# Hybrid decoder step on one core: TensorE's order within an expert step, gathered row's sums ahead of the front piece

## The reference, cut to what matters

```python
q, k, v, u = project(x, w_in)
a = diff_attention(q, k, v, ...)        # 4 heads, causal; the sample group reads 8 pages of cached K and V a sequence
s = s5_mixer(u, ...)                    # state space model, then a gated linear unit (GLU)
x1 = layer_norm(ALPHA * x + concat(a, s) @ w_out)
# PEER: per token 8 heads, each picks 16 of 16384 experts
q = rms_norm(x1 @ w_q); s = q @ sub_keys; best, idx = top-k of sums of two top-16 lists
act = gelu(einsum('thkd,td->thk', u_tab[idx], x1))
f = einsum('thk,thkd->td', softmax(best) * act, v_tab[idx])
y = layer_norm(ALPHA * x1 + f)
```

## Time and profile before

| | |
|---|---|
| median of 3 runs | 3472.05 us (3468.49 to 3473.14) |
| profiled execution | 3468.09 us, of it span 3466.3 us |
| PE busy | 2588.0 us (75%) |
| DVE busy | 2387.7 us (69%) |
| ACT busy | 1510.9 us (44%) |
| POOL busy | 1258.6 us (36%) |
| mean granted TensorE clock | 0.821 |
| gathers (POOL, L1139) | 1088 of 1 MB, 1140.92 MB of 1314.04 MB moved |
| chain that ended last | DMA 32%, PE 26%, DVE 24%, ACT 8%, issue 7% |

### The profile page before, as it was taken

The page is one execution under the profiler, slowest core; times in us unless marked ns, Lnnn a source line. Parts: engine busy times, 40 slices in busy tenths (PEclk is TensorE's granted clock), DMA queues, the critical chain, the costliest instruction groups (busy, mean ns, idle before and its releaser), DMA issues.

```text
span 3466.3 us, 44430 instructions
## 1 busy us (share of the span) xinstructions
PE 2588.0 (75%) x14196; PEld 1078.2 (31%) x14196; DVE 2387.7 (69%) x5442; ACT 1510.9 (44%) x4355; POOL 1258.6 (36%) x1100
## 2 busy tenths in 40 slices
PE   8997897776777677767776687677767876778766
PEld 5664553321232123312331233123312322332311
DVE  8627754786678667876787678766876687446765
ACT  1124453435444444444444444544455444544443
POOL 0001343434443444344334443444344433224243
PEclk9998998877887778778877888789867986888966
DMA  5367999999999999999999999999999999999998
GB/s 162 82 184 289 387 416 373 421 383 420 418 421 386 417 421 417 389 415 421 421 385 415 421 421 383 410 421 418 386 406 421 409 386 401 359 381 380 415 364 336
DMA packets 245201, 1314.04 MB, mean 379 GB/s; under 512 B 50871, under 2 KB 72151, under 8 KB 94555
## 3 DMA queue, kind: packets, MB, share of 16 engines
q0 software_dynamic: 156672, 1140.92, 80.7%
q1 hardware_dynamic: 74576, 158.28, 12.5%
q10 hardware_dynamic: 13722, 12.01, 1.1%
HBM read 1291.83 MB, written 17.97 MB: 378 GB/s over the span
## 4 chain that ended last, share of the span: by engine, by line
DMA 32%; PE 26%; DVE 24%; ACT 8%; issue 7%; POOL 1%; SPq 1%; DVEq 0%; POOLq 0%; ACTq 0%
DMA UV<-in_peer_uv,zone_x 27%; PE psum L1363 10%; DVE zone_z L1721 10%; PE psum L389 3%; PE psum L1264 3%; PE psum L529 2%; DMA wq<-in_cache_k 2%; ACT L1474 2%; DVE zone_x L1618 1%; DVE zone_x L1619 1%; DVE zone_x L1621 1%; ACT D L1479 1%; DVE zone_x L1620 1%; ACT wge L1476 1%; ACT zone_y L1374 1%
## 5 line engine op out<-in xcount | busy, mean ns | idle before, releaser
L1139 POOL DMA_INDIRECT UV<-in_peer_uv,zone_x x1088 | 1253.0, 1152 | 2105.4 <-PE psum L1363 1763.9
L1363 PE MATMUL psum<-UV,D 64*64 64x512 f32 x8704 | 1431.1, 750 | 761.5 <-ACT D L1479 708.1
L1721 DVE CUSTOM_DVE_ANT_0 zone_z<-UV,zone_x 128x1024 bf16<-128x1024 f32 x1088 | 1333.7, 1226 | 711.1 <-DMA UV<-in_peer_uv,zone_x 647.7
L1474 ACT ACTIVATE ge<-acts 128x1 f32<-128x1 f32 x1088 | 219.3, 202 | 1456.8 <-DVE acts L1721 1452.6
L1363 PEld LDWEIGHTS psum<-UV,D 64*64 64x64 f32 x8704 | 301.0, 155 | 1537.2 <-issue 1470.0
L1479 ACT ACTIVATE D<-id,wge 128x64 f32<-128x64 f32 x1088 | 378.4, 348 | 35.4
L1476 ACT ACTIVATE wge<-ge,zone_x 128x1 f32<-128x1 f32 x1088 | 320.6, 295 | 35.4
L1293 PE MATMUL psum<-wq,zone_z 128*128 128x256 f32 x1024 | 288.6, 432 | 1.2 <-ACT zone_z L1415 1.2
L1293 PEld LDWEIGHTS psum<-wq,zone_z 128*128 128x128 f32 x1024 | 209.5, 215 | 149.7 <-issue 116.9
L1474 ACT ACT_TABLE_LOAD x115 | 147.5, 1283 | 2.4 <-ACT vrows L661 0.4
L1264 PE MATMUL psum<-w_out_sb,zone_z 128*128 128x512 f32 x256 | 128.8, 626 | 17.9 <-DMA w_out_sb<-in_w_out 17.9
(11 more groups left out here) (305 smaller groups left out, 2285.1 us busy)
## 6 DMA issues: line engine op xcount, KB each, us to landing
wq<-in_peer_w_q SPq DMA_DIRECT2D x72, 1024.0 KB, 9.5
UV<-in_peer_uv,zone_x POOLq DMA_INDIRECT x1088, 11.7
wq<-in_cache_k SPq DMA_DIRECT2D x64, 256.0 KB, 8.3
vrows<-in_cache_v SPq DMA_DIRECT2D x64, 256.0 KB, 6.0
wq<-in_w_in SPq DMA_DIRECT2D x11, 1024.0 KB, 5.4
zone_x<-in_x_all SPq DMA_DIRECT2D x9, 512.0 KB
UV<-in_w_out SPq DMA_DIRECT2D x2, 2048.0 KB, 12.3
w_out_sb<-in_w_out SPq DMA_DIRECT2D x1, 4096.0 KB, 17.7
```

What stands on the lines that cost most here:

```text
L1139: pool.indirect_dma_start(out=UV[:, n % RING, :], out_offset=None, in_=table, in_offset=bass.IndirectOffsetOnAxis(ap=icur[:, t % 2, k:k + ...
L1363: ins = pe.matmul(bank[6 + r][q:q + 64, :], D[64 * r:64 * r + 64, n % RING, :], UV[64 * r:64 * r + 64, n % RING, DM + 512 * e:DM + 512 * e ...
L1474: act.activation(ge[:, j:j + 1], acts[:, j:j + 1], ACT.Gelu).then_inc(sem("gelu_done"), 1)
L1721: dve.tensor_tensor_reduce(out=junk[:, :], in0=UV[:, n % RING, 0:DM], in1=x1[:, t % 2, :], scale=1.0, scalar=0.0, op0=ALU.mult, op1=ALU.ad ...
```

## The change

PE's body of an expert step is turned round: the sums of step k first, then the front pieces of step k. `pe_finish` and `pe_unit` still follow both. Nothing else changes: the same instructions, semaphores, slots and transfers, and the order on DVE, ACT, POOL and SP stays.

```diff
@@ -1838,9 +1838,9 @@
                     pe_front(pe, 0, f)
                 for t in range(NT + 1):
                     for k in range(steps(t)):
+                        pe_expert(pe, t, k)
                         for u, f in fronts(t, k):
                             pe_front(pe, u, f)
-                        pe_expert(pe, t, k)
                         if t and k in (6, 11):
                             pe_finish(pe, t - 1, (6, 11).index(k))
                         i = unit_at_step(t, k, 0)
```

## The result

The changed kernel takes 3620.12 us (median of 3 runs, 3618.36 to 3627.26) against 3472.05: 148 us longer, a ratio of 1.044 (95% interval 1.0423 to 1.0457). It was forecast slower at 3569, +97 us, with a range of 3508 to 3645. The profiled execution has a span of 3618.3 us, against 3466.3.

The account below looks back on a forecast made before the run. DMA gathers were taken to bound the kernel after start-up, with the sample front's engine chain nearly level. Terms 85 (sample front) + 5 (tile 0) + 7 (prompt tiles) = +97 on the profiled 3468.1 gave 3565, median 3569; range 3508 to 3645.

Parts of the forecast that it names:

- The block sum, 39.6 us: Sample front: one sequence's loop over steps r = 0 to 5, 34.7 us plus 4.9 for low clock, against 24.1 now.
- The ring at the full clock: Sample front: closed loop PE, ACT, PE, ACT without overlap, DVE closing it in r = 4 and 5; 34.7 us a sequence.
- first and last block: Sample front's end blocks: first without exponentials, map or values, an estimated 29 us; last without keys, an estimated 20.
- Prompt tiles, +1 us a tile: Prompt tiles: ACT waits 0 to 2 us per head, nearly all absorbed; +7 us in all, bounds -8 and +40.
- the rival's mechanism, `sc_ready`: Prompt tiles: ACT's waits pass to DVE through `sc_ready`, 56 us instead of 7, giving 3618; chance 0.12.
- My sign of being wrong: Prediction wrong if sample blocks stay under 30 us or prompt tiles move by more than 5 us each.
- my sign of being right: Outside the sample stage, prompt tiles keep their length within 2 us.
- Tile 0, +5 us: Tile 0's first steps: GLU matmuls start some 4.8 us later, ACT and DVE need them; +5 us, bounds 0 and +15.
- The low clock throughout: Sample stage: clock stays low, all PE work on the path doubles, stage 415 us, result 3658; chance 0.10.
- Hidden: Sample stage: the loop is hidden behind transfers, stage stays at 241 us, result 3472 to 3479; chance 0.05.
- faster: Tiles' starts: earlier sums release slots earlier, worth 7 us a tile, 50 in all; result 3440 to 3465, chance 0.03.
- smaller loop: Sample stage: a smaller loop, for instance sums rarely waiting for the diagonal in r = 3 to 5; 3480 to 3510, chance 0.05.

Follow-up runs that it names:

- the run with ACT's copies later: Turned order only beside the sample front, with ACT copying the transposed K pages one piece later, against the kernel before: 3501.72 us against 3468.91, ratio 1.0110.
- The experiment: Kernel before, with only the two query projection pieces of each head in prompt tiles moved behind the sums: 3463.78 us, ratio 0.9999.
- the experiment of the first ten steps: Kernel before, with the turned order only in the first ten steps of tile 0: 3469.97 us against 3464.52, ratio 0.9999.
- the sample-only run: Kernel before, with the turned order only beside the sample front (steps 31 to 84 of tile 7): 3564.88 us against 3465.62, ratio 1.0299.

## Why the prediction held, point by point

**Bound and direction.** Right. The DMA engines are at 90% or more from slice 5 on (the last slice of the earlier trace rows is at 8 tenths, which I had read as 90%), no instruction changed, and yet a stage whose full blocks had DMA at 0.92 to 1.02 became an engine chain with DMA at 0.65 to 0.76 (forecast near 0.65).

**The block sum, 39.6 us.** Measured 39.0 to 41.5, 40.5 in the mean (3278.3 less 2994.5, by 7). By steps, from the ends of the diagonals of the block shown, with the forecast at the clock assumed for each:

| | forecast | measured |
|---|---|---|
| r = 0, low clock | 7.7 + 1.7 = 9.4 | 9.4 |
| r = 1, low clock | 5.9 + 3.2 = 9.1 | 8.0 |
| r = 2, full clock | 6.1 | 7.6 |
| r = 3, full clock | 3.9 | 5.0 |
| r = 4 and 5 | 11.1 | 11.4 |

The mechanism and the full-clock part are right, but that the block came out within 3% is partly luck. The ring at the full clock gives 34.7 us. The other 6 us are for the most part the clock, and I had put it partly into the wrong steps. In r = 1 doubling all PE work was too much: keys and map took 3.9 us (3125.86 to the copies at 3129.79) in place of 4.8 and a hand-over of 0.2. My PE work of that step was also added up 0.2 short: the terms give 3.4, not 3.2. In r = 2 and 3 I had assumed the full clock. But the values ran slow, so that 3.84 us passed from their start to the keys in place of 2.23, and in r = 3 sums and keys took 1.55 and 1.97 in place of 1.09 each. By step the errors are -1.1, +1.5, +1.1 and +0.3 us.

**The term that was mis-sized: first and last block.** Forecast 29 and 20 us, measured 32.7 and 25.5, 9 us together. The last block has no keys, and I took it as open for that reason (18.6 plus a little). It isn't: values (r = 2) now start behind their sums, and DVE waits for them in r = 3:

```profile
3294.30 1.43 DVE L1550 TENSOR_SCALAR zone_y<-psum,small 32x128 f32<-32x128 f32 x4 [10.44 <-PE psum L1215]
```

In the first block the key transposes took 1.97 us in all four steps, where I had put in little for the clock. The DMA engines stand at 1.02 there, but they do so as well in the run with ACT's copies later, where this block took 26.1 us, which speaks for the ring as what set its length. The seven full blocks add the other 7 us (283.8 against 277). The stage came to +101 us against +85. Against the 235.4 us that six kernels with the old order take there in the mean, it is +107.

**Prompt tiles, +1 us a tile.** This is the step that failed. Measured +5 a tile against the kernel before, 29 us, and +4 against the mean of the six kernels with these tiles unchanged (353.9). I looked at the query projection because it is the longest piece that ACT waits for. The experiment puts its price at 0. The loss came through the rival's mechanism, `sc_ready`: key scores, ACT's copy, DVE's top-k. That chain ends at DVE, at 84 of 100 us busy in those stretches, and I had the numbers for it. I priced the rival at 56 us and gave it 0.12: its way was right and its size twice too large. My sign of being wrong, prompt tiles that move by more than 5 us each, just did not come true (4.9 in the mean), and my sign of being right, within 2 us, failed. The result lies 55 us above the forecast by the profiled spans: 16 of them in the stage, 22 in the prompt tiles, 7 in tile 0's first steps, 10 in the rest. So 3620 lies above my forecast's own 3510 to 3615, and only the wider range holds it.

**Tile 0, +5 us.** Not contradicted. The two profiles show 12 us, the experiment of the first ten steps nothing that it could tell from noise, and the scatter between like kernels is 7 us. The mean of the three turned kernels is 139.3 us, that of nine kernels with the old order 133.8.

**The rest.** 101 + 29 + 12 makes 142 of the 152 us between the profiled spans. Of the other 10, 4 lie in tile 0 behind its first 34 steps, 5 in steps 85 to 127 of tile 7 and 1 in tile 8. The 5 are more than scatter: those steps take 137.9 to 138.9 us in the three kernels that turn them and 131.5 to 134.5 in the others. No run took them apart. The step intervals around a tile boundary do not grow (17.3 us for four in the mean, 19.5 before).

**Rivals.** The low clock throughout did not come: the granted clock of the full blocks is 0.71 to 0.80, and the sums of r = 4 and 5 run at 1.09 us. Hidden, faster and smaller loop are out by the sample-only run (+99). On transposes and the clock the traces stay undecided. In the new loop eight of them take 1.97 us or 1.09. In r = 0 they are slow in every full block, right behind slow sums, and in r = 2 fast in every one, right behind the values, so that no step sets them apart from PE's other work.

**The other signs.** ACT's waits for L1183 became the rule, as forecast, but 48 in place of 32, with 2.4 us each: where the transposes are slow, ACT waits for each of the two copies. DVE's wait at L1539 grew (49.3 to 74.8 us), and PE waited for the diagonal in 44 of 54 steps. The key transposes of r = 3, which were to be fast, were so in two of seven blocks.

## What to carry to other kernels

When engines run one list of pieces side by side, note for each hand-over how many steps lie between giver and taker, and in which order the giver has its pieces and the work that waits for the taker. A hand-over within one step is free only while the giver runs ahead; turned round it becomes a ring. Its price is at least the plain sum of durations around the ring, which one timeline of the kernel before gives (34.7 of 40.5 us here). The rest was PE's lower clock (granted 0.71 to 0.80 in the full blocks, 0.75 to 0.90 before), and that part I could only bound. Look for the loss at the engine that is nearly full and at what it waits for, not at the longest piece: ACT's extra 31 us of waiting cost nothing, with DVE's extra 50 us the time grew by 30.

## What the runs showed that I had not expected

- A wait of the engine that is nearly full is not all cost. Taking 28 us off DVE's wait for the scores in the old kernel only moved them to its wait for gathered rows, and the time rose by 0.26%. With PE one step further ahead 34 us went the same way, and the time did not change.
- PE's clock fell not only after gaps of 5.6 us and more. In the block shown the values ran slow (3.47 us in place of 1.95 at 3011.80, granted clock 0.50 from 3133.22 to 3136.64) after a gap of 2.20 us and eight sums at 1.09. They did so in six of the seven full blocks, and the sums of r = 3 ran at 1.09 to 1.99 us from block to block.
- The sample stage of the old order varies by 15 us (228.0 to 243.0) between six kernels that are the same there. PE's waits for K and V pages differ along with it: 28 us in the two longest (241.3 and 243.0), 14 and 17 in the two shortest. A single profile of the stage is good to no more than that.
